# The retention branch's gate projection as seven quadrant products for three of its four tile pairs, with the sums of x rebuilt on VectorE

## What is computed

```python
h = rms_norm(x, g_mix[l])
proj = einsum('bld,de->ble', h, w_in[l])          # among its parts: gate_r and gate_a, 1024 columns each
merged = (sigmoid(gate_r) * (ro @ w_br_ret[l])    # ro: gated output of the retention branch, 1024 wide
          + sigmoid(gate_a) * (mo @ w_br_att[l]))
x = x + merged @ w_out[l]
```

## Time and profile before

| | us |
|---|---|
| median of 3 runs | 1979.16 (1978.31 to 1979.25) |
| the profiled execution's own time | 1980.56 |
| its span | 1978.9 |
| TensorE (PE) busy in the span | 1959.4 (99%) |
| DVE busy | 1217.7 (62%) |
| ACT busy | 849.1 (43%) |

### The profile page before, as it was taken

The page is one execution under the profiler, slowest core; times in us unless marked ns, Lnnn a source line. Parts: engine busy times, 40 slices in busy tenths (PEclk is TensorE's granted clock), DMA queues, the critical chain, the costliest instruction groups (busy, mean ns, idle before and its releaser), DMA issues.

```text
span 1978.9 us, 41246 instructions
## 1 busy us (share of the span) xinstructions
PE 1959.4 (99%) x16851; PEld 1838.7 (93%) x16851; DVE 1217.7 (62%) x1952; ACT 849.1 (43%) x1365; POOL 133.6 (7%) x221
## 2 busy tenths in 40 slices
PE   8999999999999999999999999999999999999999
PEld 8968978999999999999998798799899999999999
DVE  6475413347445888988674743143664458889876
ACT  4365522332224354555434754233332344555544
POOL 0001120011000000000000012200110000000000
PEclk9999999999999999999999999999999999999999
DMA  6327683245334343333344277812443342433332
GB/s 211 125 69 220 203 286 99 86 150 168 121 108 131 86 130 91 103 106 89 106 156 131 86 217 234 284 56 91 166 146 112 98 137 79 132 107 104 89 113 83
DMA packets 254563, 262.55 MB, mean 133 GB/s; under 512 B 13706, under 2 KB 218674, under 8 KB 253874
## 3 DMA queue, kind: packets, MB, share of 16 engines
q1 hardware_dynamic: 235186, 190.69, 31.2%
q0 software_dynamic: 19072, 69.22, 10.7%
q10 hardware_dynamic: 128, 0.15, 0.0%
HBM read 234.98 MB, written 25.03 MB: 131 GB/s over the span
## 4 chain that ended last, share of the span: by engine, by line
PE 93%; DVE 4%; ACT 1%; issue 1%; DMA 1%; POOLq 0%; POOL 0%; DVEq 0%; ACTq 0%
PE PS L804 38%; PE PS L1221 21%; PE PS L784 3%; PE PS L939 3%; PE PS L785 3%; PE PS L786 3%; PE PS L764 2%; PE PS L765 2%; PE PS L766 2%; PE PS L979 2%; PE PS L1025 1%; PE PS L709 1%; PE PS L917 1%; PE PS L887 1%; PE PS L901 1%
## 5 line engine op out<-in xcount | busy, mean ns | idle before, releaser
L1803 DVE TENSOR_TENSOR WL<-RAW,WH 128x2048 fp32r<-128x2048 f32 (+2 forms) x88 | 188.7, 2144 | 116.8 <-ACT WH L1315 116.7
L804 PE MATMUL PS<-XH,WH 128*128 128x272 f32 x1152 | 243.1, 292 | 0.6
L804 PE MATMUL PS<-XL,WH 128*128 128x272 f32 x1152 | 238.0, 288 | 0.0
L804 PE MATMUL PS<-XH,WL 128*128 128x272 f32 x1152 | 237.9, 288 | 0.0
L804 PEld LDWEIGHTS PS<-XH,WH 128*128 128x128 f32 x1152 | 180.6, 188 | 7.8 <-issue 5.2
L804 PEld LDWEIGHTS PS<-XL,WH 128*128 128x128 f32 x1152 | 181.0, 189 | 0.0
L1315 ACT ACTIVATE WH<-RAW 128x2048 fp32r<-128x2048 f32 (+2 forms) x96 | 172.6, 1798 | 19.2 <-PE PS L804 18.6
L804 PEld LDWEIGHTS PS<-XH,WL 128*128 128x128 f32 x1152 | 180.4, 189 | 0.0
L1221 PE MATMUL PS<-KQ,CH 128*128 128x272 f32 x1088 | 158.3, 288 | 1.4 <-DVE KQ L2251 1.4
L784 PE MATMUL PS<-WH,XH 128*128 128x256 f32 x512 | 152.1, 297 | 0.0
L1221 PEld LDWEIGHTS PS<-KQ,CH 128*128 128x128 f32 x1088 | 145.0, 188 | 2.2 <-issue 2.2
(11 more groups left out here) (427 smaller groups left out, 4926.4 us busy)
## 6 DMA issues: line engine op xcount, KB each, us to landing
RAW<-in_w_in SPq DMA_DIRECT2D x106, 512.0 KB, 4.7
RAW<-in_w_gu SPq DMA_DIRECT2D x128, 256.0 KB, 3.9
PG<-in_cache_k SPq DMA_DIRECT2D x64, 256.0 KB, 3.3
PG<-in_cache_k POOLq DMA_DIRECT2D x64, 256.0 KB, 3.4
RAW<-in_w_down SPq DMA_DIRECT2D x64, 256.0 KB, 3.9
RAW<-in_w_gu SPq DMA_DIRECT2D x24, 512.0 KB, 5.1
PG<-in_cache_v SPq DMA_DIRECT2D x44, 256.0 KB, 3.5
PG<-in_cache_v POOLq DMA_DIRECT2D x44, 256.0 KB, 4.2
```

The source lines that it names most:

```text
L804: last = pe.matmul(PS[:, 2 * pair + h, 0:HALF], w[:, i, c0:c0 + P], block[:, h * HALF:(h + 1) * HALF], start=first and i == 0 and a == 0, ...
L1803: dve.tensor_tensor(WL[:, slot, 0:n], RAW[:, slot, 0:n], WH[:, slot, 0:n].bitcast(F32), ALU.subtract).then_inc(lo_ready, 1)
```

## The change

Of the four gate units of the stage the first stays. The other three become three steps g = 0 to 2 of seven quadrant products (`gr_seven`), and they now stand one behind the other, behind the first odd unit; the other three odd units follow them. SyncE loads each of the three as four pieces (two per semaphore) of 128 columns in place of two pieces of 256. The sums of x need x as plain float32, which no longer exists at this point; DVE adds XH and XL quadrant by quadrant (`whole`, four instructions) into XR, makes four sums in place there (`x_sum`), ACT copies their high parts to SH1 to SH4, DVE their low parts into SL (`x_low`). The sigmoids of later tiles are kept in SG until their odd unit comes. The first odd unit behind the steps is split in two halves (`half_high`, `half_low`). The loops become plain code.

```diff
+            def whole(r, c):
+                dve.tensor_tensor(x_quad(XR, r, c), x_quad(XH, r, c).bitcast(F32), x_quad(XL, r, c).bitcast(F32),
+                                  ALU.add).then_inc(x_whole, 1)
+            whole(1, 1)
+            whole(0, 1)
             ahead("br_ret", 0, 0)
...
-            branch_ret(0)
-            with own.loop(3, 0) as i:
-                branch_ret(i + 1)
...
+            whole(0, 0)
+            x_sum(1, (1, 1), (0, 1), (1, 1), ALU.add)
+            x_sum(2, (0, 1), (0, 0), (0, 1), ALU.subtract)
+            x_sum(3, (0, 0), (1, 1), (0, 0), ALU.subtract)
+            whole(1, 0)
+            x_sum(4, (1, 0), (0, 0), (1, 0), ALU.subtract)
+            for m in range(2):
+                scaled(T0["br_ret"] + m, m, EA[:, m, :])
+            gr_a_low(0)
+            gr_sums(0)
+            x_low(1, 1, 1)
+            x_low(2, 0, 0)
+            gr_t12_low(0)
+            x_low(3, 0, 1)
+            x_low(4, 1, 0)
+            for m in range(2):
+                merged(0, m, T0["br_ret"] + 2 + m, 2 + m, EB[:, m, :])
+            gr_t34_low(0)
+            merged_low(0)
+            merged_low(1)
+            gr_a_low(1)
+            gr_sums(1)
+            gr_t12_low(1)
+            for g in range(NGR - 1):
+                gr_second(g)
+                gr_t34_low(g + 1)
+                gr_first(g)
...
```

On PE (a step with its waits), and on ACT:

```diff
             unit2(U0["br_ret"] + 1, 1, T0["br_ret"] + 2, kk, (ROH, ROL))
-            with pe.Fori(1, 4) as i:
-                unit2(U0["br_ret"] + 2 * i, 0, T0["br_ret"] + 4 * i, kk, x)
-                unit2(U0["br_ret"] + 2 * i + 1, 1, T0["br_ret"] + 4 * i + 2, kk, (ROH, ROL))
...
+                pe.wait_ge(gr_la, lay * NGR + g + 1)
+                pe.wait_ge(tile_free, lay * NT + tile)
+                product(1, a_chunk("11"), a_bank, start=True).then_inc(gr_prod, 1)
+                pe.wait_ge(gr_l12, lay * NGR + g + 1)
+                product(2, t_chunk(pair12, t1), f_bank, start=True).then_inc(gr_prod, 1)
+                pe.wait_ge(gr_copied, lay * (4 * NGR) + 4 * g + 1)
+                product(3, t_chunk(pair12, t2), a_bank).then_inc(gr_prod, 1)
+                product(4, a_chunk("21"), c_bank).then_inc(gr_prod, 1)
+                split_ready(U0["br_ret"] + 2 + g)
+                pe.wait_ge(gr_copied, lay * (4 * NGR) + 4 * g + 3)
+                product(5, t_chunk(pair34, 0), a_bank).then_inc(gr_prod, 1)
+                product(6, a_chunk("22"), f_bank).then_inc(gr_prod, 1)
+                pe.wait_ge(gr_copied, lay * (4 * NGR) + 4 * g + 4)
+                product(7, t_chunk(pair34, 1), a_bank).then_inc(tile_done, 2)
...
+            sig(T0["br_ret"], 0, 0, 0)
+            gr_a_high(0)
...
+            for n, (r, c) in enumerate(((1, 1), (0, 0), (0, 1), (1, 0)), 1):
+                act.wait_ge(xs_sum, lay * 4 + (1, 3, 2, 4)[n - 1])
+                act.activation(SH[n - 1][:], x_quad(XR, r, c), ACT.Copy).then_inc(xs_hi, 1)
+                if n == 2:
+                    gr_t12_high(0)
+            sig(T0["br_ret"] + 1, 1, 1, 0)
```

More of the change, by code:

```diff
@@ L81 @@
 NPAIR = NQ // 2
+NGR = 3
 HK = KT // 2
@@ L388, in t34, with gr_a, gr_t12, gr_t34 @@
         return FIRST34[low][:] if s == 0 else CH[:, 7:16:8] if low else T34H[:]
+    def gr_a(g, low):
+        return CH[:, 8 * low + 2 * (g % 2):8 * low + 2 * (g % 2) + 3]
+    def gr_t12(g, low):
+        return T12G[:] if not low else CH[:, 13:15] if g else CH[:, 3:12:8]
+    def gr_t34(low):
+        return CH[:, 7:16:8] if low else CH[:, 5:7]
     def value_of(f):
@@ L533, in _, with gr_quad @@
             run("rg", w_in, C_RG, 2)
-            with sp.Fori(0, 4) as i:
-                full(U0["br_ret"] + 2 * i, 0, w_in, KT, C_GR + i * UC)
-                full(U0["br_ret"] + 2 * i + 1, 1, w_br_ret, KT, i * UC)
+            full(U0["br_ret"], 0, w_in, KT, C_GR)
+            full(U0["br_ret"] + 1, 1, w_br_ret, KT, 0)
+            for g in range(NGR):
+                dst, at_c = raw_chunks(g % 2), w_chunks(g % 2)
+                def gr_quad(name):
+                    r, c = int(name[0]) - 1, int(name[1]) - 1
+                    col = C_GR + (g + 1) * UC + c * P
+                    return (dst[:, at_c[name], :].rearrange("p (k c) -> p k c", c=P),
+                            rows(w_in, r * HK, HK)[:, :, col:col + P])
+                unit(U0["br_ret"] + 2 + g, g % 2, [gr_quad("11"), gr_quad("22")])
+                for name in ("21", "12"):
+                    d, c = gr_quad(name)
+                    sp.dma_start(d, c).then_inc(landed_gr[g % 2], 16)
+            for i in range(1, 4):
+                full(U0["br_ret"] + 4 + i, i % 2, w_br_ret, KT, i * UC)
             run("out", w_out, 0, 2)
@@ new lines, in _ @@
+            for g in range(NGR):
+                gr_seven(g)
+            pe.wait_ge(half_lo, lay + 1)
+            for m in range(2):
+                feature_tile(T0["br_ret"] + 10 + m, 2 + m, 1, UC, m * P, kk, (ROH, ROL), final=False, part=kk[:4])
+            split_ready(U0["br_ret"] + 5)
+            for m in range(2):
+                feature_tile(T0["br_ret"] + 10 + m, 2 + m, 1, UC, m * P, kk, (ROH, ROL), first=False, part=kk[4:])
+            for i in range(2):
+                unit2(U0["br_ret"] + 6 + i, i, T0["br_ret"] + 12 + 2 * i, kk, (ROH, ROL))
@@ L1553, in _ @@
             act.wait_ge(st_out, lay * 16 + 16)
[L1554 to L1564, removed]
@@ L1569, in _ @@
+            act.wait_ge(landed[1], (lay * NU // 2 + (U0["br_ret"] + 5) // 2 + 1) * 32)
+            half_high(0)
+            gr_step_done(NGR - 1)
+            half_high(1)
+            gr_sig(6)
+            gr_sig(7)
+            for i in range(1, 4):
+                split(U0["br_ret"] + 5 + i, (i + 1) % 2, 8 * UC, (tile_done, lay * NT + T0["br_ret"] + 8 + 2 * i))
+                merged_high(2 * i)
+                merged_high(2 * i + 1)
             with act.Fori(0, 2) as i:
@@ L2146, in _ @@
             dve.wait_ge(x_lo, lay * NX + X0["rg"] + KT)
[L2148 to L2166, removed]
@@ new lines, in gr_first, with merged @@
+            def gr_first(g):
+                dve.tensor_tensor(halves(EA[:, 0, :]), pair[2 * (g % 2)], RB, ALU.mult).then_inc(tile_free, 2)
+                dve.wait_ge(gr_up, lay * (2 * NGR) + 2 * g + 1)
+                dve.tensor_tensor(EA[:, 1, :], EA[:, 1, :], RSTDB[:], ALU.mult).then_inc(gr_up, 1)
+            def merged(i, m, tile, p, gate):
+                k = 2 * i + m
+                dve.wait_ge(sig_done, lay * NSIG + (S0N["br_ret"] + k + 1 if i == 0 else S0N["br_ret"] + KT))
+                done(tile)
+                dve.tensor_tensor(halves(EA[:, m, :]), pair[p], halves(gate), ALU.mult).then_inc(tile_free, 1)
+                dve.wait_ge(tile_free, lay * NT + tile + 3)
+                dve.tensor_tensor(G1[:, k, :], G1[:, k, :], EA[:, m, :], ALU.add).then_inc(val_ready, 1)
@@ new lines, in _ @@
+            gr_a_low(0)
[5 more added lines that the diff above has]
+            x_low(4, 1, 0)
+            for m in range(2):
+                merged(0, m, T0["br_ret"] + 2 + m, 2 + m, EB[:, m, :])
[9 more added lines that the diff above has]
+                gr_first(g)
+                if g + 2 < NGR:
+                    gr_a_low(g + 2)
+                    gr_sums(g + 2)
+                    gr_t12_low(g + 2)
@@ L2172, in residual @@
+            half_low(0)
+            gr_second(NGR - 1)
+            half_low(1)
+            gr_first(NGR - 1)
+            for i in range(1, 4):
+                split(U0["br_ret"] + 5 + i, (i + 1) % 2, 8 * UC)
+                for m in range(2):
+                    merged(i, m, T0["br_ret"] + 8 + 2 * i + m, 2 * (i % 2) + m, SG[:, 2 * i + m, :])
+                    merged_low(2 * i + m)
             def residual(tile, p, k, gcol, hi, squared, back=None):
```

153 lines of the change are left out of this document (150 added, 3 removed).

## The result

The changed kernel takes 1993.1 us (median of 4 runs, 1992.53 to 1993.16), the kernel before on the same chip 1979.2 us (4 runs, 1978.31 to 1979.31). The ratio is 1.0071 [1.0053, 1.0088]: 13.9 us slower. The forecast was 1988.9 with a range from 1984.5 to 1994.0. So the sign was right and the time lies in the range, but the forecast slowdown of 9.7 us was 4.2 us too small.

What follows compares the result with a forecast made beforehand. PE was taken to bound the kernel; 8.8 us of waits on DVE's queue against 4.0 saved gave 4.9 us more a layer, 9.7 in both: 1979.16 + 9.7 = 1988.9 us, range 1984.5 to 1994.0.

Steps and rivals of the forecast that it cites:

- What bounds the kernel, and the saving of PE: Gate stage: PE is the bound; three units of 11.99 us become steps of 10.66, saving 4.0 us a layer.
- `whole` at 1.29 us: DVE's additions of XH and XL: each priced at 1.29 us, after the low part of a quadrant.
- neither bound: Limits for one `whole`: 0.71 us from below (total 1986.5), 2.3 us from above (total 1997.9).
- DVE's queue and the waits: DVE's queue from 493.8 to 527.3 makes PE idle 4.8, 1.8 and 2.2 us, 8.8 us a layer.
- The 1.8 us ahead of product 5: Step 0: PE's second wait, until DVE's `gr_t34_low` ends at 518.9.
- the loss vanishes, because DVE sets 527.4: A clock fall in the first or second wait costs nothing; DVE alone times product 2 of step 1.
- the third wait: PE's wait ahead of product 2 of step 1: 2.2 us; only a clock fall from there costs, 1.7 us a layer.
- 4.9: Net slowdown a layer in us: gate steps end at 547.2 where the old units would end at 542.3.
- Rival 1: The clock falls behind PE's wait at product 2 of step 1 in each layer: 1992.3 us; chance 0.12.
- Rival 2: Wider cover, waits under 4.0 us a layer: faster, 1971.2 with none; no change half way; chance 0.15.
- Rival 3: Step 2's 128-column pieces land late, 1.5 us a layer: 1991.9 us; chance 0.06.
- Rival 4: Products cost 1.60 us each, more than in feed-forward steps, adding 1.0 us a layer: 1990.9; chance 0.05.

Runs made afterwards that it cites:

- late: Changed kernel with the gate's first remaining unit in plain form (96 matmuls), two seven-product steps, DVE's and ACT's queues fitted: 1973.98 us, ratio 0.9975; again 1973.3 us, 0.9972.
- warm2: Changed kernel with filler matmuls nobody reads in three of PE's waits, the second filler accumulating instead of starting anew: 1987.93 us, ratio 1.0049.
- nosums: Changed kernel without any work on the sums of x; the products read plain quadrants, so the gate's result differs: 1978.68 us, ratio 1.0005.
- order: Changed kernel, same instructions in another DVE and ACT order: gate tiles read out and first chunks' parts made before the sums of x: 1983.67 us, ratio 1.0027.
- nowhole: Changed kernel without the four `whole` additions of XH and XL, sums taken from XH alone: 1985.2 us, ratio 1.0032.
- warm: Changed kernel with filler matmuls in three of PE's waits, the second filler starting an accumulation anew in PSUM bank c: 1987.68 us, ratio 1.0046.

## Why the prediction was right and where it was wrong

The sum of a stage, all from rows: 83.9 - 3 x 1.45 (the saving) + 4.67 + 2.53 (waits) + 2.7 + 1.6 (what PE's work at half clock takes longer) = 91.0 us, measured 91.1. In layer 1: 83.9 - 4.4 + 7.2 + 2.4 + 1.5 = 90.6, measured 90.7.

- **What bounds the kernel, and the saving of PE:** right. PE sets the stage, and what was saved there would have shown: `late` has it. The term was 0.4 us a layer too small. The 10.66 us of a step in the feed-forward part contain small waits (in the trace before PE is busy for 41.66 of the 42 us from 820 to 862), and the forecast had the new steps keep them; they don't.
- **`whole` at 1.29 us:** measured 1.287. Taking the nearest row was right; neither bound came near.
- **DVE's queue and the waits:** right. 4.8 us forecast ahead of product 2 of step 0, 4.67 measured. The 1.8 us ahead of product 5 aren't in the trace because PE at half clock filled them: products 2 to 4 took so long that DVE was ready. At full clock (`warm2`) they are there. Without the falls (`warm2`) product 2 of step 1 stands at 32.9 us, forecast 33.0, and the kernel at 1987.9 us, forecast 1988.9. Of the 1.0 us between them the undersized saving is 0.8.
- **The clock: wrong, here are the missing 4.2 us.** The step that failed is "the loss vanishes, because DVE sets 527.4". The mechanism that failed is that overlap, and it fails in two ways. First, 527.4 wasn't DVE's alone. Its queue there contains low parts that wait for ACT, and ACT waits for PE's product 3, so PE's slow stretch moved DVE as well: product 2 of step 1 came 526.75 - 492.7 = 34.05 us behind the stage's start, 1.05 later. Second, I took no fall behind the third wait, with the argument that dense matmuls ran ahead of it. They did, and the clock fell all the same: 1.6 us, near the 1.7 of the earlier trace rows. The measured time lies in the range only because the range took this fall in as a rival; the sum didn't have it. Together 4.9 + 1.05 + 1.6 less some 0.3 for cheaper products is 7.2 us a layer, which is what the stage grew by.
- **Rival 1** (a fall behind the third wait, 1992.3 us) is what took place, with the loop's 1.05 us a layer on top, and I gave it 0.12. What spoke against it was one example at the program's start with short transposes ahead. One such row shows that a pause of 1.88 us can bring a fall; it can't show that denser work ahead protects. The page "TensorE: Matmul & The Clock Gate" of the Trainium skill, section "Part 1: The HAM clock gate (the "warmup" mystery)", calls the half rate the default state, from which only activity leads out. In both layers of the changed kernel the trace agrees: clock 0.50 behind 4.67 and behind 2.53 us. In `nosums` and `order` it doesn't always (last section).
- **Rival 2** (the cover is wider) didn't take place. Its turning point to no change, four quadrant instructions less, wouldn't have been enough either: `nosums` has twelve fewer, ten of them in that stretch, still waits 2.52 us, behind ACT, and only just comes to no change.
- **Rival 3** (narrow pieces late) is false. The issues stand at 517.32 and 518.28 on SyncE's queue, with 4.5 us to landing, and ACT, which wants them at 526.61, doesn't wait for them. **Rival 4** is false: products are cheaper than said (10.56 us for seven, 1.51 each), not dearer.

SyncE's queue and the landing time of the pieces (from the window 500 to 560), to which this refers:

```profile
517.32 0.92 SPq L512 DMA_DIRECT2D RAW<-in_w_in  x2
518.28 1.06 SPq L572 DMA_DIRECT2D RAW<-in_w_in  x2
```

```profile
RAW<-in_w_in SPq DMA_DIRECT2D x4, 256.0 KB, 4.5
```

## What to carry to other kernels

Before matmuls are exchanged for work of other engines, write out those engines' queues up to the first matmul that needs the result: a stage in which DVE is half idle can still be 5 us late at that one point, and starting the scheme one unit later, with the queues fitted to it, for two steps in place of three, turned 13.9 us of loss into 5.6 us of gain. Follow such a queue through every engine it waits for, back to PE itself: if the chain closes, a delay of PE isn't absorbed by the wait behind it. And price a fall of the clock behind each new wait of PE as likely, not as a rival: in the traces here it came in or behind 14 of 16 waits of 2.0 to 4.7 us, and each fall took 1.5 to 3.0 us of full-speed matmul time, of which waits that follow can take up a part.

## What was not expected of the hardware

The same wait doesn't always have the same effect on the clock. In `nosums` PE waits 2.52 us at the same instruction in both layers, with the same matmuls ahead. In layer 0 the clock stays at full, in layer 1 it falls:

```profile
519.00:522.00 3.00, 1.96 (x15) 1.00 0.00 0
522.00:525.00 3.00, 3.00 (x26) 1.00 0.63 214
...
1489.00:1492.00 3.00, 1.35 (x9) 0.93 0.00 0
1492.00:1495.00 3.00, 3.00 (x15) 0.50 0.41 138
```

In `order` it is so too with the wait of 3.07 us: 1.00 from 510 to 516, but 0.65, 0.50 and 0.71 in the windows from 1486 to 1495. Yet in the trace of `nowhole` waits of 1.98 to 2.26 us bring a fall each of the four times. So the length of a wait alone doesn't decide; what does, these runs don't settle.

Nor does the fall have to come inside the wait. In `nowhole` PE's first wait ends at 509.39, and the clock drops only when PE has been at work again for 1.6 us:

```profile
510.00:511.00 1.00, 1.00 (x10) 0.98 0.00 0
511.00:512.00 1.00, 1.00 (x7) 0.50 0.00 0
```

And the same kernel doesn't always have the same falls. The mean clock of `nowhole` is 0.995 in the traced execution and 0.997 in the five others, which are 0.2 to 2.9 us faster. That of `nosums` is 0.998 in two executions (1976.74 and 1977.34 us) and 0.996 or 0.997 in eight (1977.76 to 1983.81). A kernel with waits of some 2 to 3 us thus has a time that spreads by chance, and a trace shows one case of it; in the changed kernel, with 4.67 and 2.53 us, all four executions have 0.994.

A second point is on PSUM. In `warm` matmuls that start an accumulation anew in unread columns of bank c changed the computed values; in `warm2`, where the same matmuls only accumulate, they didn't. Columns that the kernel reads lie in the same bank: there product 4 accumulates onto ACT's copy of product 1, in step 0 and again in step 2. Which value was lost was not looked at.
